# Where TensorE's products with the values stand in a slot of the attention stage

## The reference

```
v_new = val_c - kcd_c @ S
o_c   = qg_c @ S + intra_c @ v_new
S     = S * exp(gl_c) + kend_c^T @ v_new
```

```
logits = (q @ k^T) * scale + cum[q] - cum[k]      # causal
p = softmax(logits);  o = p @ v
```

## Time and profile before

| | |
|---|---|
| median of 3 runs | 1612.64 us |
| profiled execution | 1609.38 us, its span 1607.6 us |
| mean granted TensorE clock | 0.984 of full speed |
| `mix` in the span | 817 to 1413 us |

### The profile page before, as it was taken

One profiled execution on the slowest core, in us unless ns is written; L12 is line 12 of the kernel. 1 busy time (PEld: TensorE's weight loads), 2 busy tenths in 40 slices (PEclk: granted clock), 3 DMA queues, 4 the chain that ended last, 5 costly groups with the idle time before them and its releaser, 6 DMA issues. The chain is left out here.

```text
span 1607.6 us, 22182 instructions
## 1 busy us (share of the span) xinstructions
PE 1547.3 (96%) x7890; PEld 1224.3 (76%) x7890; DVE 923.3 (57%) x1436; ACT 691.5 (43%) x1307; POOL 622.6 (39%) x540
## 2 busy tenths in 40 slices
PE   7999999999999999999979999998999999979998
PEld 6888888888888888888856676666766677667886
DVE  7464555555317766901256776666667676545755
ACT  0436363645411111131125776765676777830100
POOL 1212021211311111111036787877786887911111
PEclk9999999999999999999979999999999999989999
DMA  6134344252573334226544645453546455324642
GB/s 254 49 118 144 96 119 128 88 156 72 157 117 125 131 118 131 72 70 140 158 136 130 186 118 148 141 145 93 145 125 180 119 149 169 88 76 115 200 138 92
DMA packets 190657, 206.49 MB, mean 128 GB/s; under 512 B 50940, under 2 KB 134140, under 8 KB 187516
## 3 DMA queue, kind: packets, MB, share of 16 engines
q1 hardware_dynamic: 189972, 203.24, 44.2%
q10 hardware_dynamic: 576, 1.84, 0.4%
HBM read 129.79 MB, written 75.17 MB: 127 GB/s over the span
## 5 line engine op out<-in xcount | busy, mean ns | idle before, releaser
L1487 POOL TENSOR_TENSOR m_p_lo<-m_p,m_p_hi 128x512 fp32r<-128x512 f32 (+1 forms) x320 | 373.9, 1190 | 61.1 <-ACT m_p_hi L1451 59.7
L545 PE MATMUL bank<-x_hi,w_hi 128*128 128x512 f32 x992 | 394.3, 397 | 0.0
L545 PE MATMUL bank<-x_hi,w_lo 128*128 128x512 f32 x992 | 387.1, 390 | 0.0
L545 PE MATMUL bank<-x_lo,w_hi 128*128 128x512 f32 x992 | 386.2, 389 | 0.0
L570 POOL TENSOR_TENSOR w_lo<-w_raw,w_hi 128x512 fp32r<-128x512 f32 x64 | 92.9, 1473 | 481.0 <-ACT w_hi L628 481.0
L1449 ACT ACTIVATE m_p<-m_st,fcol 128x512 f32<-128x512 f32 (+1 forms) x320 | 204.2, 638 | 153.9 <-PE m_st L1336 77.3
L1539 DVE TENSOR_REDUCE m_maxima<-m_aux 128x1 f32<-128x512 f32 (+2 forms) x320 | 195.3, 619 | 122.1 <-PE m_aux L1311 73.6
L545 PEld LDWEIGHTS bank<-x_hi,w_lo 128*128 128x128 f32 x992 | 186.2, 188 | 40.1
L545 PEld LDWEIGHTS bank<-x_lo,w_hi 128*128 128x128 f32 x992 | 186.6, 188 | 36.4
L545 PEld LDWEIGHTS bank<-x_hi,w_hi 128*128 128x128 f32 x992 | 186.4, 188 | 36.2
L1451 ACT ACTIVATE m_p_hi<-m_st,fcol 128x512 fp32r<-128x512 f32 (+1 forms) x320 | 202.5, 633 | 0.0
(11 more groups left out here) (204 smaller groups left out, 2522.3 us busy)
## 6 DMA issues: line engine op xcount, KB each, us to landing
w_raw<-in_w SPq DMA_DIRECT2D x31, 512.0 KB, 3.9
dram_feat<-ring SPq DMA_DIRECT2D x48, 256.0 KB, 4.2
arena<-dram_gates SPq DMA_DIRECT2D x32, 256.0 KB, 4.9
o_y<-dram_mixT SPq DMA_DIRECT2D x16, 512.0 KB, 6.1
o_x<-in_x SPq DMA_DIRECT2D x16, 512.0 KB, 4.1
out<-o_res SPq DMA_DIRECT2D x15, 512.0 KB, 5.0
arena<-in_xT SPq DMA_DIRECT2D x7, 1024.0 KB, 8.7
K<-dram_k_hi SPq DMA_DIRECT2D x12, 512.0 KB, 7.2
```

The costliest lines, as they stand in the source:

```text
L545: mm = pe.matmul(banks[bank_of(s)][:], w[:, i % 2, k * P:(k + 1) * P], x[:, k, b * BLOCK:(b + 1) * BLOCK], start=(k == 0 and n == 0), stop ...
L1487: pool.tensor_tensor(p_lo[(s - 1) % PL][:, off:], p[(s - 1) % PL][:, off:], p_hi[(s - 1) % PH][:, off:].bitcast(F32), ALU.subtract).then_i ...
```

## The change

In the loop of TensorE the call of `values` is moved behind `do_aux` and `chain`. A slot then runs S, A, C, V. Nothing is added or removed, no semaphore or buffer is changed, and the loops of the other engines are as before.

```
                 for s in range(END_SLOT + 1):
                     if s < N_UNITS:
                         scores(s)
-                    if 0 <= s - LAG < N_UNITS:
-                        values(s - LAG)
                     for item in AUX_AT.get(s, ()):
                         do_aux(item)
                     if s in CHUNK_AT:
                         chain(*CHUNK_AT[s])
+                    if 0 <= s - LAG < N_UNITS:
+                        values(s - LAG)
```

## The result

The changed kernel takes 1634.98 us in the median of 4 runs (1632.33 to 1641.66), the kernel before 1612.72 us (1612.24 to 1614.11). The ratio is 1.0143, 95% interval 1.0109 to 1.0176: 22.3 us, 1.4%, slower. I had forecast 1610.6 us and a range up to 1617.5. The profiled execution of the changed kernel took 1632.88 us, its span 1631.1.

A forecast was written before the change was run, and what follows sets the result against it. TensorE's order of work was taken to set the pace (busy 565.5 of 596 us). Gains of 4.0 and 3.0 less a loss of 5.0 made 2.0 us gained: 1612.6 to 1610.6 us, range 1603.5 to 1617.5 (8 in 10).

The forecast's parts named there:

- (3): In 31 group-ending slots VectorE's `finish` is delayed by A + C, 18 us in all; 5.0 us lost on TensorE.
- near 1.8 us: Forecast sign: TensorE's wait behind slot 214, 1.12 us before, grows by 0.67 us.
- 0.23 later costs nothing: Claim for slot 94, where a group ends: VectorE has spare time enough, so the delay of 0.23 us costs 0.
- a rival, with 7.9 us at the most: Ends of the groups win: delayed `finish` costs 12.6 us in 12 slots with a step; 7.9 us slower, 1620.5; chance 0.20.
- (1): TensorE's neighbours: V instead of S behind short matmuls hides weight loads better; 4.0 us gained, bounds 0 and 8.9.
- The rule of the Trainium skill: On TensorE weight loads overlap matmuls only where row groups differ; this would make (1) 0 instead of 4.0 us.
- (2): Longer distance from S to its V shortens TensorE's waits for `p_lo`; 3.0 us gained, bounds 0 and 4.1.
- GpSimd's wait for V: GpSimd's `p_lo` waits for V of the unit three before, ending about when `p_hi` is there; cost set to 0.
- (4): What stays: the slot 144 stop, SyncE's waits, before and behind `mix`, last slots, all 0; clock only widens the range.
- the clock: Halved-clock stretches of 3.2 us and 2.0 us in `mix` may come or go, about 3 us either way.

The follow-up runs named there:

- e2: Kernel before, with the order S, A, C, V only in the 32 slots where V is the last of its group: 1629.29 us, ratio 1.0119.
- e1: Changed kernel, but the 32 slots where V is the last of its group keep the old order S, V, A, C: 1622.02 us, ratio 1.0068.
- e3: Changed kernel, with `finish` behind A's and C's work of the same slot on VectorE: 1613.00 us, ratio 1.0007 to the kernel before.
- e13: Changed kernel, with `finish` behind A's but in front of C's work on VectorE: 1614.95 us, ratio 1.0009 to the kernel before.
- e8: V between A and C in every slot (S, A, V, C), against the kernel before: 1638.06 us, ratio 1.0156.
- e14: Order S, A, V, C with `finish` behind A's and C's work on VectorE, against the kernel before: 1617.92 us, ratio 1.0035.
- e5: Kernel before (S, V, A, C), with `finish` behind A's and C's work of its slot on VectorE: 1608.04 us, ratio 0.9973.
- e9: Kernel before, with `finish` behind A's but in front of C's work on VectorE: 1605.82 us, ratio 0.9959.
- e4: Changed kernel with four buffers of `p` and `p_lo` instead of three: 1637.46 us, ratio 1.0168 to the kernel before.
- e12: e3 with four buffers of `p` and `p_lo` instead of three: 1612.11 us, ratio 1.0000 to the kernel before.
- e7: e1 with each row of maxima issued one slot later: 1638.27 us, ratio 1.0139 to the kernel before.
- e6: Kernel before with each row of maxima issued one slot later: 1618.15 us, ratio 1.0033.
- e11: Changed kernel, with `finish` behind A and C of the next slot on VectorE: 1611.56 us, ratio 0.9992 to the kernel before.
- e10: Kernel before, with `finish` behind A and C of the next slot on VectorE: 1610.38 us, ratio 0.9985.

## Why the prediction was wrong

**(3), the end of a group, is the step that failed.** It named the right place and mechanism and got the delay wrong. I wrote that `finish` is delayed by A + C of its slot. But before, V *ended* where A began, and the next slot's V stood in front of the next A. After, V ends behind A, C and V itself, and only S stands between it and the next A. What `finish` loses against the next A is A + C + 0.7 us, in each of the 31 slots: 18 + 22 = 40 us in all instead of 18. The 0.7 has two halves. V of a finishing slot has 256 columns and takes 0.35 us, and the next A comes 0.35 us sooner behind its predecessor, because this short V stands between them and no longer the V of 512 columns of the next group.

In slot 214 the wait grew by 1.39 us (1.12 to 2.51), where I said 0.67: A is 0.67, V of that slot 0.35 (1250.44 to 1250.79), the sooner next A 0.35. `finish` itself took as long as before (1.42 and 1.43 us from its start to the copy). The sign that I gave, "near 1.8 us", is what e2 shows, where the delay is A + C alone, and e1 adds the 0.7 on its own.

Going through the 31 slots of the trace of before again in the same way, with A + C + 0.7, the delay is larger than VectorE's spare time in 18 slots instead of eight, and the sum is an estimate of 16 to 17 us instead of 6.5. TensorE's waits for the two banks rose by 14.9 us (14.0 to 28.9), where I had said about 5. In e2 they rose by 6.5 us, so the walk through the slots was good and the delay put into it was not. Slot 94's "0.23 later costs nothing" was 0.94 later against the next A. I saw the shape of this loss as a rival, with 7.9 us at the most; with the same missing 0.7 us its price was too low as well.

**What is shown of it.** That the loss goes through VectorE's queue, A's results behind `finish`: e3 and e13 give it back without touching TensorE. That both parts of the delay count: the waits of e1 (V without A + C), e2 (A + C without V) and the changed kernel (both); e8 with e14 says the same of V. That the kernel before paid some of it: e5 and e9.

**(1), the neighbours.** Half of the reasoning held. V behind a 128-column mask 0.26, A behind the scores' mask 0.32, S 0.23. But I had carried the 0.26 over from a mask in bfloat16 to a step in float32, where no row showed it: V behind a step takes 0.32, so the 6.4 us of the 128 steps weren't there (behind E1 and E2 it is 0.28 instead of 0.34, 32 x 0.06 = 1.9 us). The sum is 2.5 + 1.9 - 4.2, about 0 instead of 4.0.

The rule of the Trainium skill (TensorE: Matmul & The Clock Gate, The mechanism), by which weight loads overlap only across row groups, gives 0 for this term too. The same section names a background weight buffer as a second case in which a load is pulled ahead, which I left out; that sentence does not forbid what the rows show. The rows after still speak against the rule as I quoted it: 0.23 us from one full-array matmul to the next, 0.32 behind a short one. That the term came out near 0 is no point for it, since it did so by gains and losses of 2 to 4 us that cancel.

**(2), from S to V.** Right in what it looked at: the waits for `p_lo` fell from 4.1 to 1.0 us. GpSimd's wait for V, which I had set to 0 because the times meet, became 69 us of waits; as a cost it is indeed about 0 (e4, e12).

**(4), what stays, is the second step that failed: the clock was no mere spread.** The stop at slot 144 stayed (3.9 us). The clock did not: the granted clock shows 37 us of `mix` at the lower level (1.2 GHz) before and 58.0 after. Fully busy, TensorE loses half of such time, so this is at most 10.6 us of the 25. About 3 of the 21 us more lie at the start of the stage, in a stretch that lasts between 17 and 27 us in the traces of this case, whatever the order; 15.6 lie in the finishing slots and the three behind them. The four runs of the changed kernel have mean granted clocks of 0.972 to 0.980, with a mean of 0.977; those of the kernel before, over all experiments, 0.979 to 0.987 and 0.983. After slot 215's wait of 2.51 us the clock was at the lower level for part of the next 4 us:

```profile
1254.00:1258.00 4.00, 4.00 (x17) 2.98 (x18) 2.28 (x7) 0.47 (x1) 1.27 (x1) 0.66 0.08 27
```

The window is from 1254 to 1258 us of the changed kernel, its columns as in the earlier trace rows. I had the clock as a spread of 3 us either way. Here it came with the waits: the mean over the runs is lowest, 0.975 to 0.977, where the waits for the banks are longest (e4, e7, e8 and the changed kernel, 25.7 to 35.1 us), and highest, 0.985, in e9, with 9.9 us. It does not follow their sum alone: e6 has 22.9 us of them at 0.983, the clock of the kernel before. So I count it to the price of the waits in this change, as an estimate; no run held the clock fixed.

**The sum again.** With (1) at 0, (2) at 3 gained, (3) at 17 lost and 11 lost to the clock, it is 25 us slower, against 22.3 by the medians and 25.5 in the pair of profiles. That it comes so near is in part luck: (3) and the clock are estimates, each good to a few us.

**What stays open.** With `finish` in the same place, the new order still costs something: e3 against e5 0.34%, e13 against e9 0.50%, but e11 against e10 0.07%. One reading was the rows' waits for GpSimd's `max_diag`, since V no longer gives it time between S and A. They are longer in every pair, by 2.6, 4.2 and 2.9 us (10.5 to 13.1, 8.5 to 12.7, 4.4 to 7.3). But the last pair shows no loss, so they are a part at most. e6 and e7 were to test this and did not, because the rows landed in finishing slots. What they are a part of may be TensorE's waits as a whole, rows and banks: in the three pairs of profiles these are longer by 5.0, 6.1 and 1.9 us (39.6 to 44.6, 38.3 to 44.4, 40.5 to 42.4), in the order of the losses. So it is argued, not shown. e1 and e2 together cost 26.1 us, more than the 22.3 of the whole; the difference is about as large as the intervals allow, and I can't say whether the two parts add up.

## What to carry to other kernels

When a step is moved behind others on one engine, write down where it ended before and where it ends now, and measure both to the next use of what is being waited for: the step moves by the others, and its own length no longer stands between it and that use. Then go to each engine that waits for that end, and ask what stands behind the waiting instruction in its queue: a result that is ready and has a bank of two to free must be taken out before the wait, not behind it. Here that rule, applied to the kernel before (e9), was worth 0.41% on its own, and in the changed one it took a loss of 1.4% down to 0.1% (e3, e13). And look at the granted clock when a wait is priced: here about 15 us of longer waits came with a loss of 22.

## What the runs showed of the hardware

From the first to the second matmul of 512 columns it took 0.26 us where the first has a 65-column weight load and stands behind a bfloat16 mask of 128 columns, and 0.32 us where it stands behind a float32 step of the recurrence (1296.56 and 1182.52 of the changed kernel); with a 128-column load it took 0.32 behind either. So the smaller load was worth 0.06 us behind the mask and nothing that can be measured behind this step. The length of the matmul ahead does not settle it alone: behind a mask of 256 columns the 65-column load had 0.32 as well. A float32 step, shown as eight matmuls of 128 columns, took 0.81 us.

The granted clock fell to its lower level (1.2 GHz) behind a wait of TensorE of 2.51 us (slot 215 of the changed kernel; 0.66 on the mean from 1254 to 1258 us), and `mix` had 58.0 us of that level where the kernel with shorter waits had 37.
